# Gate products in fp32r, tiles made between VectorE's two splits, gelu one block late, decode halves added by VectorE

## The reference

```
q = (xf @ wq).reshape(t, PEER_HEADS, PEER_QDIM)          # router, 8 heads
top_s, pos = lax.top_k(cand_s, PEER_TOPK)                # 16 of 16384 experts a head
expert = ...reshape(t, -1)                               # 128 experts a token
gate = softmax(top_s)
z = einsum('cd,ced->ce', xc, u[ec])                      # up
act = gelu(z, approximate=False) * gate
out = einsum('ce,ced->cd', act, v[ec])                   # down
```

## Time and profile before

| | |
|---|---|
| median of 3 runs | 2789.86 us (2789.66 to 2791.29) |
| profiled execution | 2789.84 us, its span 2787.9 us |
| TensorE busy | 2744.4 us, 98%; its weight loads 2366.5 us, 85% |
| VectorE, ScalarE, GpSimd busy | 65%, 51%, 12% |
| granted TensorE clock | 0.996 of full speed |
| chain that ended last | TensorE 73%, issue 21%, GpSimd 2%, VectorE 2%, ScalarE 1% |
| DMA | 514.76 MB, 185 GB/s on average |

### The profile page before, as it was taken

How to read it: one execution, slowest core, us unless ns; L and a number is a source line. 1 busy time by engine, 2 the same in 40 slices (tenths; PEclk the granted TensorE clock), 3 DMA queues, 4 the chain that set the end, 5 groups by cost and what they waited for, 6 DMA issues and landing times.

```text
span 2787.9 us, 48242 instructions
## 1 busy us (share of the span) xinstructions
PE 2744.4 (98%) x14688; PEld 2366.5 (85%) x14688; DVE 1818.3 (65%) x2903; ACT 1409.1 (51%) x2067; POOL 342.3 (12%) x438
## 2 busy tenths in 40 slices
PE   8999999999999999999999999999999999999998
PEld 6888878888888888888888999888888888888887
DVE  6666665668986666579995666666665555555555
ACT  5455545556665444466655544555554444444444
POOL 0000000000001110011126996000000000000000
PEclk9999999999999999999999999999999999999999
DMA  6544455564554444555555445666665555555564
GB/s 244 190 156 162 150 169 187 177 218 159 173 179 160 158 155 140 195 183 192 191 195 176 156 158 162 214 214 209 214 206 196 195 190 195 192 192 195 191 238 158
DMA packets 153554, 514.76 MB, mean 185 GB/s; under 512 B 17056, under 2 KB 33696, under 8 KB 152480
## 3 DMA queue, kind: packets, MB, share of 16 engines
q1 hardware_dynamic: 131904, 480.44, 52.2%
q10 hardware_dynamic: 21600, 33.70, 3.4%
HBM read 501.49 MB, written 12.58 MB: 184 GB/s over the span
## 4 chain that ended last, share of the span: by engine, by line
PE 73%; issue 21%; POOL 2%; DVE 2%; ACT 1%; DMA 0%; POOLq 0%; SPq 0%; DVEq 0%; ACTq 0%
PE bank L509 21%; PE bank L514 11%; PE bank L2249 8%; PE bank L2251 8%; PE bank L2250 8%; PE bank L547 3%; PE bank L549 3%; PE bank L548 3%; PE bank L2224 2%; POOL big L634 2%; DVE w_lo L469 1%; PE bank L492 1%; PE bank L494 1%; PE bank L493 1%; PE bank L2082 0%
## 5 line engine op out<-in xcount | busy, mean ns | idle before, releaser
L469 DVE TENSOR_TENSOR w_lo<-raw,w_hi 128x1024 fp32r<-128x1024 f32 x904 | 1105.7, 1236 | 796.2 <-ACT w_hi L460 791.0
L460 ACT ACTIVATE w_hi<-raw 128x1024 fp32r<-128x1024 f32 x904 | 951.4, 1059 | 933.0 <-PE bank L2251 373.2
L509 PE MATMUL bank<-act,w_hi 128*128 128x512 f32 x3840 | 980.7, 397 | 5.4 <-ACT big L984 1.9
L509 PEld LDWEIGHTS bank<-act,w_hi 128*128 128x128 f32 x3840 | 692.0, 189 | 136.2 <-issue 7.8
L514 PEld LDWEIGHTS bank<-act,w_lo 128*128 128x128 f32 x3840 | 523.3, 190 | 39.4 <-DVE w_lo L469 0.8
L514 PE MATMUL bank<-act,w_lo 128*128 128x256 f32 x3840 | 535.1, 282 | 0.1
L2249 PE MATMUL bank<-w_hi,expert_act 128*128 128x512 f32 x1008 | 392.2, 389 | 0.1
L2250 PE MATMUL bank<-w_lo,expert_act 128*128 128x512 f32 x1008 | 392.1, 389 | 0.0
L2251 PE MATMUL bank<-w_hi,expert_act 128*128 128x512 f32 x1008 | 392.1, 389 | 0.0
L2249 PEld LDWEIGHTS bank<-w_hi,expert_act 128*128 128x128 f32 x1008 | 189.3, 188 | 39.6 <-DVE cst L525 0.5
L2251 PEld LDWEIGHTS bank<-w_hi,expert_act 128*128 128x128 f32 x1008 | 189.3, 188 | 39.3
(11 more groups left out here) (308 smaller groups left out, 2603.3 us busy)
## 6 DMA issues: line engine op xcount, KB each, us to landing
raw<-in_stream SPq DMA_DIRECT2D x904, 512.0 KB, 3.3
big<-in_ukv ACTq DMA_DIRECT2D x16, 512.0 KB, 4.6
z_kept<-cst ACTq DMA_DIRECT2D x64, 128.0 KB, 3.1
cst<-z_kept ACTq DMA_DIRECT2D x64, 128.0 KB, 3.8
big<-in_x SPq DMA_DIRECT2D x2, 1024.0 KB, 9.6
big<-in_rows ACTq DMA_DIRECT2D x2, 1024.0 KB, 8.3
big<-in_rg_w ACTq DMA_DIRECT2D x1, 2048.0 KB, 11.0
x_kept<-big ACTq DMA_DIRECT2D x1, 2048.0 KB, 6.7
```

What stands on the lines that cost most here:

```text
L460: act.activation(w_hi[:, s, :], raw[:, s, :], ACT.Copy).then_inc(hi_ready, 1)
L469: dve.tensor_tensor(w_lo[:, s, :], raw[:, s, :], w_hi[:, s, :].bitcast(F32), ALU.subtract).then_inc(lo_ready, 1)
L509: pe.matmul(bank[:, :], w_hi[:, s, kk * P:(kk + 1) * P], act2[:, k, :, :].rearrange("p a n -> p (a n)"), start=(k == 0), stop=False)
```

## The change

- Each token's product is of fp32r tiles. `hot` holds the one-hot tile of the second index. `weighted` holds the first index's one-hot tile twice, times the gate's high part and times its low part (`scalar_tensor_tensor`, 256 columns). The product's two halves, in banks 0, 1 or 4, 5, are joined in `G`: ScalarE copies the low one, VectorE adds the high one (`add_gates`).
- The gates stage has 64 pairs with four tokens each, between the w_hi and the w_lo products of a pair's second unit (`between`); the late stage has 32 blocks. The number of up blocks stays. 96 blocks go over `z_kept`, and 64 of them come back during the first 32 turns of the experts.
- VectorE makes the tiles for the next block between its two splits. ScalarE makes a block's gelu in the next block's turn.
- In decode, `low_half` and `add_halves` join the halves; GpSimd has no part in it. TensorE waits for the sum of two blocks before (`wait_summed`), and ahead of the stage for all copies of the router.

```diff
-         ("wqu", 4 * PH), ("u_decode", 2 * PH), ("u_gates", S // 8), ("u_late", NB // 2), ("v", NB)]
-EARLY = NB // 2
+         ("wqu", 4 * PH), ("u_decode", 2 * PH), ("u_gates", S // 4), ("u_late", NB // 4), ("v", NB)]
+EARLY = 3 * NB // 4
...
-        hot = sb("hot", [P, 2, 4, P])
+        weighted = sb("weighted", [P, 4, 2, P], F32R)
+        with nc.sbuf_tensor("below_hot", [P, CONST["causal"][0]], F32), \
+                nc.sbuf_tensor("hot", [P, 4, P], F32R) as hot:
...
+        first_index = slot_t[:, 0, :]
+        second_index = par[:, 0:S]
+        gate_hi = slot_t[:, 1, :]
+        gate_lo = slot_t[:, 2, :]
+        GATE_BANKS = [[banks[0], banks[1]], [banks[4], banks[5]]]
...
+                if u and between:
+                    between()
                 pe.wait_ge(lo_ready, 2 * pair + u + 1)
...
-            with pool.Fori(0, PH) as i:
-                for n in range(2):
-                    add_copied(Z_HALVES[:, n, 0:S], Z_HALVES[:, n, :], i * 2 + (4 * PH + n))
...
                 keep_query(0)
+                if not first:
+                    save_early(h - 1, 1, (h - 1) * 4 + 3)
...
                 ahead(split_hi, act, "wqu", h, 4, 3)
-                early(pair_of("wqu", h, 4, 3), h, 1, h * 4 + 3, 4)
...
+                save_early(h, 0, h * 4 + 2)
+                keep_early(pair_of("wqu", h, 4, 3), 1, h * 4 + 3, 4)
...
                 for n in range(2):
-                    ahead(split_hi, act, "u_decode", i, 2, n)
-                    early(pair_of("u_decode", i, 2, n), i + PH, n, i * 2 + (4 * PH + n), 2)
...
+                    ahead(split_hi, act, "u_decode", i, 2, n, units=(0,))
+                    if first and not n:
+                        save_early(PH - 1, 1, 4 * PH - 1)
+                    else:
+                        save_decoded(i, n - 1)
+                    act.wait_ge(unit_done, 2 * pair_of("u_decode", i, 2, n) + 2)
+                    act.wait_ge(z_saved[n], i * 16 + (16 * PH + 1))
+                    low_half(act, GZ[:, n, :], banks[2 + n])
+                    ahead(split_hi, act, "u_decode", i, 2, n, units=(1,))
+
+            def save_decoded(i, n):
+                wait_summed(act, block_of("u_decode", i, 2, n))
+                act.activation(GZ[:, n % 2, :], GZ[:, n % 2, :], ACT.Gelu).then_inc(gelu_ready[n % 2], 1)
+                act.wait_ge(gelu_ready[n % 2], i + (PH + 2 + n // 2))
+                act.dma_start(z_kept[bass.ds(i * 2 + (2 * PH + n), 1), :, :].rearrange("o p n -> (o p) n"),
+                              GZ[:, n % 2, :]).then_inc(z_saved[n % 2], 16)
...
+            act.wait_ge(slots_kept, 3)
+            act.activation(gate_hi.bitcast(F32R), gate_lo, ACT.Copy).then_inc(slots_kept, 1)
             early_turn(PH - 1)
-            act.wait_ge(slots_kept, 3)
+            save_decoded(PH - 1, 1)
...
                     ahead(split_hi, act, "u_gates", i, 2, n, units=(0,))
-                    keep_gates(0)
+                    if not (first and not n):
+                        save_gelu(i, n - 1)
+                    for half in range(2):
+                        act.wait_ge(hot_used[2 * half + 1], i * 2 + n + 2)
+                        act.activation(G[:, :, bass.ds(i * 8 + (4 * n + 2 * half), 2)],
+                                       GATE_BANKS[n][half].rearrange("p (t a b) -> p a b t", t=2, a=2)[:, 1, :, :],
+                                       ACT.Copy).then_inc(gate_low, 1)
                     ahead(split_hi, act, "u_gates", i, 2, n, units=(1,))
                     act.wait_ge(unit_done, 2 * pair_of("u_gates", i, 2, n) + 2)
                     act.wait_ge(z_saved[n], i * 16 + (32 * PH + 1))
                     low_half(act, GZ[:, n, :], banks[2 + n])
...
+            with act.Fori(0, (EARLY - LATE) // 2) as i:
+                for n in range(2):
+                    act.wait_ge(early_ready[n], i + (LATE // 2 + 1))
+                    act.dma_start(GB[:, n, :], z_kept[bass.ds(i * 2 + (LATE + n), 1), :, :]
+                                  .rearrange("o p n -> (o p) n")).then_inc(z_back[n], 16)
+                next_experts(i)
...
+            def next_low(unit):
+                pair, u = unit // 2, unit % 2
+                ahead(split_lo, dve, "u_decode", 0, 2, pair, units=(u,))
+                if u:
+                    add_halves(dve, GZ[:, pair % 2, :], banks[2 + pair % 2], block_of("u_decode", 0, 2, pair))
...
+            def add_gates(i, n):
+                for half in range(2):
+                    dve.wait_ge(gate_low, i * 4 + (2 * n + half + 1))
+                    dest = G[:, :, bass.ds(i * 8 + (4 * n + 2 * half), 2)]
+                    high = GATE_BANKS[n][half].rearrange("p (t a b) -> p a b t", t=2, a=2)[:, 0, :, :]
+                    dve.tensor_tensor(dest, dest, high, ALU.add).then_inc(gate_kept[n], 1)
+
+            def four_tiles(i, n):
+                for s in range(4):
+                    tok = i * 8 + (4 * n + s)
+                    dve.wait_ge(hot_used[s], i * 2 + n + 1)
+                    dve.scalar_tensor_tensor(
+                        out=weighted[:, s, :, :], in0=iota.unsqueeze(1).broadcast_to([P, 2, P]),
+                        scalar=first_index[:, bass.ds(tok, 1)],
+                        in1=slot_t[:, 1:3, bass.ds(tok, 1)].broadcast_to([P, 2, P]),
+                        op0=ALU.is_equal, op1=ALU.mult).then_inc(hot1, 1)
...
                 for n in range(2):
-                    for s in range(8):
-                        tok = i * 16 + (8 * n + s)
-                        dve.wait_ge(hot_used[s % 4], i * 4 + (2 * n + s // 4) + 1)
-                        dve.tensor_scalar(hot[:, 0, s % 4, :], iota, slot_t[:, 0, bass.ds(tok, 1)],
-                                          slot_t[:, 2, bass.ds(tok, 1)], ALU.is_equal, ALU.mult).then_inc(hot1, 1)
-                        if s % 4 == 3:
-                            ahead(split_lo, dve, "u_gates", i, 2, n, units=(s // 4,))
+                    ahead(split_lo, dve, "u_gates", i, 2, n, units=(0,))
+                    if not (last and n):
+                        four_tiles(i, n + 1)
+                    ahead(split_lo, dve, "u_gates", i, 2, n, units=(1,))
                     add_halves(dve, GZ[:, n, :], banks[2 + n], block_of("u_gates", i, 2, n))
+                    add_gates(i, n)
...
+            four_tiles(0, 0)
...
+                    next_expert(i, n)
+                    dve.wait_ge(z_back[n], i * 16 + (8 * LATE + 16))
+                    back = G[:, bass.ds(i * 2 + (LATE + n), 1), :].rearrange("p o n -> p (o n)")
+                    dve.tensor_tensor(back, GB[:, n, :], back, ALU.mult).then_inc(early_ready[n], 1)
...
+            pe.wait_ge(copied, 4 * PH + 4)
...
-                    pe.wait_ge(copied, i * 2 + (4 * PH + n + 3))
+                    wait_summed(pe, block_of("u_decode", i, 2, n - 2))
                     halves_out(pe, pair_of("u_decode", i, 2, n), n, banks[2 + n])
...
-            with pe.Fori(0, S // 16) as i:
+            def four_tokens(i, n):
+                pe.wait_ge(gate_kept[n], i * 2 + 1)
+                pe.wait_ge(hot1, i * 8 + (4 * n + 4))
+                pe.wait_ge(hot2, i * 8 + (4 * n + 4 + 1))
+                for s in range(4):
+                    pe.matmul(GATE_BANKS[n][s // 2][:, (s % 2) * S:(s % 2 + 1) * S], hot[:, s, :],
+                              weighted[:, s, :, :].rearrange("p a b -> p (a b)"), start=True, stop=True)\
+                      .then_inc(hot_used[s], 1)
+
+            with pe.Fori(0, S // 8) as i:
                 for n in range(2):
                     pe.wait_ge(gelu_ready[n], i + (2 * PH + 1))
...
+                    halves_out(pe, pair_of("u_gates", i, 2, n), n, banks[2 + n], between=lambda: four_tokens(i, n))
```

More of the change, by code:

```diff
@@ L984, in copy_halves, with keep_early, save_early @@
                 act.activation(dest, bank[:, :], ACT.Copy).then_inc(copied, 1)
-            def early(pair, b2, n, block, before):
+            def keep_early(pair, n, block, before):
                 copy_halves(Z_HALVES[:, n, :], banks[2 + n], pair, block, before)
+            def save_early(b2, n, block):
                 act.wait_ge(z_saved[n], b2 * 16 + 1)
@@ L994, in early, with router_turn @@
                    .then_inc(z_saved[n], 16)
-            with act.Fori(0, PH) as h:
+            def router_turn(h, first=False):
                 def keep_query(a):
@@ L1090, in next_experts @@
                     expert_hi(i * 2 + (2 + n), n, 2 * pair_of("v", i, 2, n) + 2)
-            with act.Fori(0, NB // 2 - 8) as i:
+            with act.Fori(0, (EARLY - LATE) // 2) as i:
[4 more added lines that the diff above has]
+                next_experts(i)
+            for n in range(2):
+                act.wait_ge(early_ready[n], EARLY // 2 + 1)
+            with act.Fori((EARLY - LATE) // 2, NB // 2 - 8) as i:
                 next_experts(i)
@@ L1722, in more @@
                     unit = next(lows)
-                    ahead(split_lo, dve, "u_decode", 0, 2, unit // 2, units=(unit % 2,))
```

(6 more changed lines are left out.)

97 lines of the change are left out of this document (50 added, 47 removed).

## The result

The changed kernel takes 2759.14 us (median of 4 runs, 2757.97 to 2760.17) against 2789.76 for the kernel before in the same comparison: ratio 0.989, with a 95% interval of 0.9878 to 0.9901. Forecast was 2763, range 2755 to 2784. The profiled execution has a span of 2758.4 us (2787.9 before).

The account below looks back on a forecast made before the run. TensorE was taken to bound the gates, late stage and experts, with VectorE full in decode. Products -23.5, entry -5.8 and decode +2.7 gave -26.6 us, span 2787.9 to 2761.3, forecast 2763 us, range 2755 to 2784.

Parts of the forecast that it names:

- Products: Gates stage: a set of four token products goes from 0.94 to 0.57 us, over 64 sets a 23.5 us gain.
- Entry: Start of the gates stage: 6.9 us lost becomes a 1.1 us wait for VectorE's tiles, a 5.8 us gain.
- Decode: Decode stage: the first pair waits for all router copies and VectorE's adds lengthen its rounds, a 2.7 us loss.
- bound of 0.50: Gates stage: lower limit in us for a set of four token products if nothing is added, gain 28 us.
- the loop's end: Old gates stage: explains the difference between 0.90 us traced for a set and 0.94 from the whole stage.
- Rival D: Larger gain: 0.50 us a set in the gates and a decode loss under 1, 2753 to 2757 us; chance 0.06.
- are one: Decode: TensorE, 3.2 us late, asks at 1401.7, when VectorE's add also ends, so the two delays count once.
- the rounds of VectorE's selection: Decode: each round serves two pairs and takes 12.1 us with two adds, against TensorE's 11.16, so it sets the pace.
- What was hidden: Gates pair: VectorE 5.2 of 6.15 us and ScalarE 4.6, both under TensorE; experts' added reloads priced 0, at most 2.
- Rival A: Gates stage: GpSimd starves behind VectorE's splits and fused tiles, TensorE waits 0.4 to 0.8 us a pair, 2789 to 2814; chance 0.12.

Follow-up runs that it names:

- The last version: Changed kernel with decode waits per bank, VectorE's decode add before its second split, and gate_lo and first four gates tiles before the last decode pair's splits: 2752.2 us.
- a kernel with the same sums and a circle in it: Changed kernel, but in the gates stage ScalarE makes a block's gelu in the same turn, right behind its low half: 2800.59 us, ratio 1.0041.

## Why the prediction was right

The parts add up to 29.7 us of gain for a forecast of 26.6, but not each as I had it: the products won 5.7 us more, the entry 0.3 more, decode cost 1.5 more, and 1.4 us (the router's end and the late stage) had no term. The total is nearer than the parts are, and that is in part luck.

**Products**, predicted -23.5: the mechanism is shown, the size was off. I took 0.57 for a set, 0.525 for the products and 0.045 for waits and the loop. It is 0.481, below even my bound of 0.50 "if nothing is added", which did not fit my own price: nothing added is 0.525. The w_lo run that I read as 0.131 a product begins right behind 512-column products, and only the first run there pays for that: eight token products behind them took 1.06 from start to start (1600.23 to 1601.29, made twice), four took 0.58 (1599.82 to 1600.40), and the w_lo run behind them 0.96 (1600.40 to 1601.36), 0.120 a product. The 0.1 was in the unit already, and four products more add 4 x 0.120, with nothing for waits. Of the 29.2 us, 26.4 are the form of the product and 2.9 the new order: I had read the loop's end in the old 0.94 and did not see that the new order sheds it. Rival D had the right set (0.50) and the wrong decode loss.

**Entry**, predicted -5.8, from 6.9 lost to 1.1: 0.76 measured, -6.1 (the terms that I listed add up to 5.4 and not to the 5.6 that I wrote, so a wait of 0.9 was due by them), and the wait is for VectorE's tile, as said (0.5 of it in the list of waits). The last version, which makes these tiles earlier and loses nothing, shows them as the cause; the kernel with the decode part undone shows the gelu and GpSimd as the old one.

**Decode**, predicted +2.7, measured +4.2: here a step failed. PE starts 3.29 late, for 3.2. But I wrote that this delay and VectorE's "are one", and let the rounds of VectorE's selection set the rest of the stage. Sixteen pairs of 5.586 and the transposes (0.65) are 90.0 us without any loss; my forecast of 95.6 put 3.2 of delay and 2.4 of rounds on top. In place of that the runs showed two things. The idle time cost the clock, 2.7 us more (1.3 in other executions), a thing that I had read in the entry and did not apply here. And VectorE's rounds bind less than I had: PE's stalls from 1399.8 on sum to about 1.1 us for my 2.4, and with a start on time the stage takes 92.2. The delay of 3.3, the clock's 2.7 and the 1.1 of stalls make the 97.2; the kernel before lost 2.9 of its own there. Where the clock took 1.3 only, the loss is 2.8, and that this meets my 2.7 is luck: two errors that cancel.

**What was hidden**: VectorE 325.8 of 379.4 us, 86%, for a predicted 5.2 of 6.15; the strided adds take 436 to 439 ns, the fused tiles have a step of 0.40 where GpSimd is quiet and of about 0.44 beside it. The experts took no more time. But the sums of busy time did not show that the late gelu carries 41 us: I named it nowhere as a term, and a kernel with the same sums and a circle in it lost more than the change had won.

**Rival A** fell, for the reason given against it and with more in hand than I gave it (1.3 us for 0.4), since the fused tiles hardly hold GpSimd off. The rule of the Trainium skill, "SBUF — State Buffer", "Who interferes with whom", would have a fused tile, with two SBUF inputs, and a GpSimd tile take turns: the shared ports are an exclusive lock, and the one that issues second waits. By the rows they do not. GpSimd's tile from 1600.53 takes 0.76, and VectorE's fused tile, issued second at 1600.74, takes 0.59 in the middle of it; the GpSimd tiles behind it take 0.84 each for 0.60. A split, on the other hand, holds a GpSimd tile to 1.64, as in the earlier trace rows. Least, median and most of VectorE's fused tiles from 1500 to 1860 us:
```profile
L1848 DVE SCALAR_TENSOR_TENSOR weighted<-cst,slot_t x236: 469/490/596, 1503.7 to 1856.9; 128x256 fp32r<-128x256 f32 x118
```
